# Four groups of two blocks, eight row buffers and half-megabyte weight units in a decoder step with PEER experts

## What is computed

```python
mod = silu(c) @ w_ada + b_ada                     # 6 vectors of 1024 for each condition
n = rmsnorm(x, g_mix) * (1 + sc1) + sh1
a_lin, a_gate, u, v, g_a, g_b = split(n @ w_in)   # 512, 512, 512, 512, 1024, 1024
a = silu(layernorm(causal_dwconv31(a_lin * sigmoid(a_gate)))) @ w_conv_out
b = (u * chunk_spatial_gate(layernorm(v))) @ w_gmlp_out
x = x + gt1 * ((sigmoid(g_a) * a + sigmoid(g_b) * b) @ w_out)
n2 = rmsnorm(x, g_ffn) * (1 + sc2) + sh2
# PEER: 8 heads, 2 x 128 keys, the 16 best of 16384 experts for each head and position
x = x + gt2 * sum_over_128_slots(softmax_gate * gelu(u_tab[eid] . n2) * v_tab[eid])
y = rmsnorm(x, g_final)
```

## Time and profile before

| | us |
|---|---|
| median of 3 runs | 3477.16 (3476.43 to 3483.25) |
| the profiled execution | 3482.56 |
| its span, from first to last instruction | 3480.8 |
| PE busy | 2028.8 (58%) |
| DVE busy | 2284.7 (66%) |
| ACT busy | 606.0 (17%) |
| POOL busy | 1220.7 (35%) |
| moved by DMA | 1231.43 MB, mean 354 GB/s |

### The profile page before, as it was taken

One profiled execution on the slowest core, in us unless ns is written; L12 is line 12 of the kernel. 1 busy time (PEld: TensorE's weight loads), 2 busy tenths in 40 slices (PEclk: granted clock), 3 DMA queues, 4 the chain that ended last, 5 costly groups with the idle time before them and its releaser, 6 DMA issues.

```text
span 3480.8 us, 27027 instructions
## 1 busy us (share of the span) xinstructions
PE 2028.8 (58%) x8700; PEld 885.6 (25%) x8700; DVE 2284.7 (66%) x5749; ACT 606.0 (17%) x1497; POOL 1220.7 (35%) x1046
## 2 busy tenths in 40 slices
PE   6998238576779533386666878733333433354333
PEld 4777204333455100033222444300000000010000
DVE  1524884875468978857865466897677676546555
ACT  1111311112121121212112121212121211111201
POOL 0000133332333344434432333345455444434442
PEclk7999659788889655598787989955555555555555
DMA  7543278988899988999998999999999999998998
GB/s 259 206 182 133 97 281 336 373 315 315 350 403 409 404 346 320 347 382 400 373 378 339 380 417 415 389 364 380 421 422 421 421 421 409 422 394 337 421 423 344
DMA packets 183773, 1231.43 MB, mean 354 GB/s; under 512 B 30496, under 2 KB 31136, under 8 KB 36176
## 3 DMA queue, kind: packets, MB, share of 16 engines
q0 software_dynamic: 148608, 1082.20, 77.2%
q1 hardware_dynamic: 35024, 147.52, 10.6%
HBM read 1220.62 MB, written 9.02 MB: 353 GB/s over the span
## 4 chain that ended last, share of the span: by engine, by line
PE 32%; DVE 29%; DMA 29%; ACT 4%; issue 3%; POOL 1%; SPq 1%; ACTq 0%; POOLq 0%; DVEq 0%
PE ps L605 18%; DMA big<-in_experts,eid 14%; DVE big L1587 9%; DMA w<-in_experts,eid 8%; PE ps L840 7%; DMA more_rows<-in_experts,eid 3%; PE ps L757 2%; ACT wd L1069 2%; DVE arena L1286 2%; DVE eid_s L1550 2%; PE ps L661 2%; DVE more_rows L1587 1%; DVE big L1228 1%; DVE wd L1602 1%; DVE arena L1548 1%
## 5 line engine op out<-in xcount | busy, mean ns | idle before, releaser
L1127 POOL DMA_INDIRECT big<-in_experts,eid x829 | 965.7, 1165 | 2121.4 <-PE ps L840 1569.2
L840 PE MATMUL ps<-big,wd 128*32 128x512 f32 x3316 | 825.7, 878 | 1051.7 <-DVE wd L1602 1043.8
L1587 DVE SCALAR_TENSOR_TENSOR big<-big,xr 128x1024 f32<-128x1024 f32 x829 | 1003.4, 1223 | 469.4 <-DMA big<-in_experts,eid 457.7
L1069 ACT ACTIVATE wd<-mask,act 128x32 f32<-128x32 f32 x1024 | 273.1, 313 | 2276.0 <-DVE big L1587 1763.0
L605 PE MATMUL ps<-big,wring 128*128 128x384 f32 (+2 forms) x1696 | 581.2, 494 | 89.1 <-issue 56.0
L840 PEld LDWEIGHTS ps<-big,wd 128*32 128x32 f32 x3316 | 94.8, 127 | 1594.2 <-DVE wd L1602 1526.2
L605 PEld LDWEIGHTS ps<-big,wring 128*128 128x128 f32 x1696 | 325.3, 198 | 360.8 <-issue 176.6
L1602 DVE TENSOR_TENSOR wd<-wd,gate 128x64 f32<-128x64 f32 x512 | 114.1, 223 | 271.1 <-ACT wd L1069 269.9
L840 PE MATMUL ps<-more_rows,wd 128*32 128x512 f32 x472 | 189.4, 891 | 141.9 <-DVE wd L1602 138.2
L1587 DVE SCALAR_TENSOR_TENSOR more_rows<-more_rows,xr 128x1024 f32<-128x1024 f32 x118 | 144.1, 1221 | 58.5 <-DMA more_rows<-in_experts,eid 57.9
L1286 DVE SCALAR_TENSOR_TENSOR arena<-arena,wdw 128x384 f32<-128x384 f32 (+1 forms) x360 | 182.2, 569 | 0.0
(11 more groups left out here) (241 smaller groups left out, 2091.1 us busy)
## 6 DMA issues: line engine op xcount, KB each, us to landing
wring<-in_w_in SPq DMA_DIRECT2D x40, 1024.0 KB
wring<-in_w_q SPq DMA_DIRECT2D x19, 1024.0 KB
big<-in_experts,eid POOLq DMA_INDIRECT x829
wring<-in_w_ada SPq DMA_DIRECT2D x12, 1024.0 KB
wring<-in_w_out SPq DMA_DIRECT2D x9, 1024.0 KB
big<-in_w_ada SPq DMA_DIRECT2D x6, 1024.0 KB, 7.0
xr<-in_w_ada SPq DMA_DIRECT2D x6, 1024.0 KB, 6.8
big<-in_w_in SPq DMA_DIRECT2D x4, 1024.0 KB, 14.0
```

The source lines that it names most:

```text
L840: mm = mmul(ps[QUAD * j:QUAD * (j + 1), half, :], wd[:, 2 * (at % 4) + jj, :], rows[jj][:, D + 512 * h:D + 512 * (h + 1)], start=(m == 0), ...
L1069: last = ac(wd[:, c + jj, :], mask[:], ACT.Gelu, scale=act[:, c + jj:c + jj + 1])
L1127: gp.indirect_dma_start(row(r), None, t["experts"], bass.IndirectOffsetOnAxis(ap=index, axis=0)).then_inc(s_row[r], 16)
L1587: last = v.scalar_tensor_tensor(out=row(r)[:, 0:D], in0=row(r)[:, 0:D], scalar=1.0, in1=x, op0=ALU.mult, op1=ALU.mult, accum_out=act[:, c: ...
```

## The change

STARTS becomes [0, 2, 4, 6]: groups of blocks 0 and 1, 2 and 3, 4 and 5, and 6 and 7 with the samples; their matmuls have 256, 256, 256 and 264 columns. There is one front more beside pairs, each now beside 128 pairs, and WIDE_AT moves from pair 320 to 384. nT, mT, the arena and the tables get smaller with the groups, and ROWS_1 goes from 7 to 8. The ring has six places of half a megabyte in place of three of one; for group 1 it has 14 in place of 7. Units of w_in and w_q are 128 columns, "out" units 256 columns; w_ada, w_out and the v columns of w_in are cut into an upper and a lower half of their rows, and both halves are awaited together. In a branch the order is in, out, in, and a gate unit's place is free when its gate matmuls are done rather than with the column block's last matmul. The planner is the same and gets other numbers.

```diff
@@ -39,10 +39,10 @@
 NSLOT = H * TOP
-RING = 3
-RING_1 = 7
-PIECE = 2048
-STARTS = [0, 2, 5]
+RING = 6
+RING_1 = RING + 8
+PIECE = 1024
+STARTS = [0, 2, 4, 6]
 NB1 = STARTS[-1]
...
@@ -51,7 +51,7 @@
 AW = max(NBG, NBL - 1) * P + W - 1
-ROWS_1, ROWS_2 = 7, 10
+ROWS_1, ROWS_2 = 8, 10
 LAST = len(STARTS)
...
@@ -301,40 +301,48 @@
 
+        def half_pieces(kind, src, i, done, count):
+            for rows in range(2):
+                pieces.append((kind, src, 2 * i + rows, done, count))
+
         def ada_pieces(lo, hi):
             for i in range(lo, hi):
                 ada_piece.append(len(pieces))
-                pieces.append(("ada", t["w_ada"], i, S["ada_mm"], i + 1))
+                half_pieces("ada", t["w_ada"], i, S["ada_mm"], i + 1)
 
 
         ada_pieces(0, 8)
         for g in GROUPS:
             ng = g.ng
             first_piece[g.n] = len(pieces)
+            for c in range(CC):
+                pieces.append(("in", w_in, 4 + c, *g.to("gate_mm", ng * (c + 1))))
+                pieces.append(("in", w_in, c, *g.to("lin_mm", ng * (c + 1))))
+            for c in range(CC):
+                pieces.append(("in", w_in, 8 + c, *g.to("u_mm", ng * (c + 1))))
             for half in range(2):
-                pieces.append(("in", w_in, 2 + half, *g.to("lin_mm", 2 * ng * (half + 1))))
-                pieces.append(("in", w_in, half, *g.to("lin_mm", 2 * ng * (half + 1))))
-            for half in range(2):
-                pieces.append(("in", w_in, 4 + half, *g.to("u_mm", 2 * ng * (half + 1))))
-            for half in range(2):
-                pieces.append(("in", w_in, 6 + half, *g.to("v_mm", g.nb)))
+                half_pieces("v", t["w_v"], half, *g.to("v_mm", g.nb))
             if g.n == 1:
                 ada_pieces(8, 16)
-            for base, wout, done in ((12, t["w_gmlp_out"], "ob_mm"), (8, t["w_conv_out"], "oa_mm")):
+            for base, wout, gated, done in ((24, t["w_gmlp_out"], "gb_mm", "ob_mm"), (16, t["w_conv_out"], "ga_mm", "oa_mm")):
                 for col in range(4):
-                    if col % 2 == 0:
-                        pieces.append(("out", wout, col // 2, *g.to(done, 2 * ng * (col + 2))))
-                    pieces.append(("in", w_in, base + col, *g.to(done, 2 * ng * (col + 1))))
-                if g.n == 1 and base == 12:
+                    pieces.append(("in", w_in, base + 2 * col, *g.to(gated, ng * (2 * col + 1))))
+                    pieces.append(("out", wout, col, *g.to(done, 2 * ng * (col + 1))))
+                    pieces.append(("in", w_in, base + 2 * col + 1, *g.to(gated, 2 * ng * (col + 1))))
+                if g.n == 1 and base == 24:
                     ada_pieces(16, 24)
             for i in range(4):
-                pieces.append(("wo", t["w_out"], i, *g.to("wo_mm", g.nb * (i + 1))))
-            for i in range(8):
-                pieces.append(("wq", t["w_q"], i, *g.to("q_mm", 2 * ng * (i + 1))))
+                half_pieces("wo", t["w_out"], i, *g.to("wo_mm", g.nb * (i + 1)))
+            for i in range(NCH):
+                pieces.append(("wq", t["w_q"], i, *g.to("q_mm", ng * (i + 1))))
 
         def piece(n):
-            k = CC if pieces[n][0] == "out" else KC
+            k = KC if pieces[n][0] in ("in", "wq") else KC // 2
             return home(n).rearrange("p (k n) -> p k n", k=k)
+
+        def rows_of(n, c):
+
+            return piece(n + c // (KC // 2))[:, c % (KC // 2), :]
 
...
@@ -350,9 +358,9 @@
                 return wring[:, slot * PIECE:(slot + 1) * PIECE]
-            if slot < RING + 2:
-                return big[:, (8 + 2 * (slot - RING)) * D:(10 + 2 * (slot - RING)) * D]
-            return xr[:, 2 * (slot - RING - 2):2 * (slot - RING - 1), :].rearrange("p a b -> p (a b)")
+            if slot < RING + 4:
+                return big[:, (8 + slot - RING) * D:(9 + slot - RING) * D]
+            return xr[:, slot - RING - 4, :]
 
...
@@ -501,20 +509,20 @@
                 load(n)
-                if pieces[n][0] == "wq" and pieces[n - 1][0] == "wo":
+                if pieces[n][0] == "wq" and pieces[n][2] == 3:
                     spill(g)
 
             def bring_x(g):
                 for b in g.blocks:
                     sp.dma_start(xn1[:, b, :], t["x"][b * P:(b + 1) * P, :]).then_inc(g.S["x_in"], 16)
 
-            for n in range(4, first_piece[2]):
+            for n in range(8, first_piece[2]):
                 with_spill(n, G1)
-                if n == 16:
+                if n == 32:
                     bring_x(GROUPS[1])
             for g in GROUPS[1:-1]:
-                for n in range(first_piece[g.n], first_piece[g.n + 1] + (3 if g.n == LAST - 1 else 0)):
-                    if n == first_piece[g.n] + 4 and g.n < LAST - 1:
+                for n in range(first_piece[g.n], first_piece[g.n + 1] + (RING if g.n == LAST - 1 else 0)):
+                    if n == first_piece[g.n] + 8 and g.n < LAST - 1:
                         bring_x(GROUPS[g.n])
...
@@ -526,9 +534,9 @@
                 sp.dma_start(x_first[0:w, b - NB1, :], t["x"][b * P:b * P + w, :]).then_inc(GL.S["x_in"], 16)
-            first_wo = max(n for n, p in enumerate(pieces) if p[0] == "wo") - 3
-            for n in range(first_piece[LAST] + 3, len(pieces)):
-                if n == first_piece[LAST] + 11:
+            first_wo = max(n for n, p in enumerate(pieces) if p[0] == "wo") - 7
+            for n in range(first_piece[LAST] + RING, len(pieces)):
+                if n == first_piece[LAST] + 16 + RING:
 
...
@@ -629,45 +638,45 @@
                     c, gi = i // ng, i % ng
-                    if i % (2 * ng) == 0:
+                    if gi == 0:
                         arrived(n)
                         arrived(n + 1)
                     if i >= 3:
                         pe.wait_ge(*g.to("a_done", i - 2))
-                    yield from tiles(n, (c % 2) * P, gi, ps[:, pair(i), 0:tg], s["gate_mm"])
-                    yield from tiles(n + 1, (c % 2) * P, gi, ps[:, pair(i) + 1, 0:tg], s["lin_mm"])
-                    if i % (2 * ng) == 2 * ng - 1:
+                    yield from tiles(n, 0, gi, ps[:, pair(i), 0:tg], s["gate_mm"])
+                    yield from tiles(n + 1, 0, gi, ps[:, pair(i) + 1, 0:tg], s["lin_mm"])
+                    if gi == ng - 1:
                         n += 2
                 yield from gap(5)
 
                 pe.wait_ge(*g.to("a_done", CC * ng))
                 for i in range(CC * ng):
                     c, gi = i // ng, i % ng
-                    if i % (2 * ng) == 0:
+                    if gi == 0:
                         arrived(n)
                     if i >= 6:
                         pe.wait_ge(*g.to("u_done", i - 5))
-                    yield from tiles(n, (c % 2) * P, gi, ps[:, 2 + i % 6, 0:tg], s["u_mm"])
-                    if i % (2 * ng) == 2 * ng - 1:
+                    yield from tiles(n, 0, gi, ps[:, 2 + i % 6, 0:tg], s["u_mm"])
+                    if gi == ng - 1:
                         n += 1
                 yield from gap(5)
 
                 pe.wait_ge(*g.to("u_done", CC * ng))
-                arrived(n)
-                arrived(n + 1)
+                for k in range(4):
+                    arrived(n + k)
                 for i, b in enumerate(g.blocks):
                     for half in range(2):
                         for c in range(KC):
                             mm = mmul(ps[0:width(b), 2 + i % 6, half * 256:(half + 1) * 256], nT[:, c, cols(b)],
-                                      piece(n + half)[:, c, :], start=(c == 0), stop=(c == KC - 1))
+                                      rows_of(n + 2 * half, c), start=(c == 0), stop=(c == KC - 1))
                             if (half, c) == (1, KC - 1):
                                 mm.then_inc(s["v_mm"], 1)
                             if c % 4 == 3:
                                 yield
-                n += 2
+                n += 4
                 if g.n == 1:
                     ada(8, 16)
-                    n += 8
+                    n += 16
                 yield from gap(12)
...
@@ -691,22 +700,21 @@
                         j, gi = i // ng, i % ng
-                        if i % (4 * ng) == 0:
-                            no = n
-                            arrived(no)
-                            n += 1
-                        if i % (2 * ng) == 0:
-                            arrived(n)
+                        if gi == 0:
+                            gate_piece = n + 2 * (j % 2)
+                            arrived(gate_piece)
+                            if j % 2 == 0:
+                                arrived(n + 1)
                         if i >= 3:
                             pe.wait_ge(*g.to(done, i - 2))
-                        yield from tiles(n, (j % 2) * P, gi, ps[:, pair(i), 0:tg], s[gate_sem])
-                        yield from tiles(no, (j % 4) * P, gi, ps[:, pair(i) + 1, 0:tg], s[out_sem], src, CC)
```

(47 more changed lines are left out.)

## The result

The changed kernel's median is 3432.9 us (3430.81 to 3434.69, 4 runs) against 3480.2 of the kernel before on the same chip: ratio 0.986, 95% interval 0.9839 to 0.9882, some 47 us less. The forecast was 3472 with 3450 to 3495 around it, and the range over all cases 3415 to 3535: the wide range held. The sum in the prediction had 5 us less than before (3475 for 3480), and 47 were measured. It also said that a measurement here can tell 7 us, so that it forecast no step that could have been told from none. 3432.9 lies outside the forecast's own range and inside that of rival 2 (3420 to 3449).

The account below looks back on a forecast made before the run. The DMA rate was taken as the limit, with the middle short of it. Group 1 432, fronts 776, 768 and 785, pairs alone 714 sum to 3475 against 3480; forecast median 3472, own range 3450 to 3495, 80% range 3415 to 3535.

Parts of the forecast that it names:

- rival 2: Front stages: buffer and units do more than forecast, so the kernel is faster, 3420 to 3449 us; chance 0.27.
- Bytes, +80: Weights: one more group reads 32 pieces of 1 MB once more, +80 us of DMA time.
- W: Loss in the fronts' matmul stretches: 22, 22 and 25 us forecast after the change.
- R: Loss in DVE-bound heads and tails of front stages: 109 us after, before 102; buffer takes 5 us per stage off.
- Stalls, 23 a front: Matmul stretches: PE's waits for weight pieces cost 23 us a front; half units with six slots remove all.
- Floors: DMA time of each front stage beside 128 pairs: 722 us, 2166 for three.
- Pairs alone: Last 132 pairs without a front: 714 us, with 3 us for two later routes otherwise hidden by ten buffers.
- Half units: Weight loads: 184 more DMA issues on SP, free except +2 us at the start; latency covered by the experts' queue.
- Rival 3: Weight loads: each unit costs DMA engine time, 184 more cost 17 us, 3489 us in all; chance 0.05.
- Group 1: First stage, without fetches: +2 us from four more SP issues ahead of the small loads, 432 us.
- The signs: Trace: fronts at 385 to 394 GB/s, no weight piece over 5 us in the chain, heads and tails all DVE.
- rival 1: Front stages: each pair still leaves DVE idle for rows as before, so slower, 3515 to 3552 us; chance 0.30.

Follow-up runs that it names:

- e6_eq_twice: The changed kernel with the routes' is_equal instruction issued twice each time; 3502.79 us, ratio 1.006 to the kernel before.
- e4_after_rows7: The changed kernel with seven row buffers instead of eight; 3474.77 us, ratio 0.9977 to the kernel before.
- e1_units: The changed kernel put back to groups [0, 2, 5] and seven row buffers, keeping the half-megabyte units; 3413.06 us, ratio 0.979 to the kernel before.
- e2_groups: The kernel before with only the groups changed to [0, 2, 4, 6]; 3545.49 us, ratio 1.0177 to the kernel before.
- e5_hist_late: The changed kernel with the four out_hist_s stores issued after all weights; 3426.73 us, ratio 0.9842 to the kernel before.

## Why the prediction was right, and which terms were off

Right was the wide range, which was drawn so that it takes in most of both rivals. The case that the forecast held likeliest (0.38, 3450 to 3495) did not come out.

- *Bytes, +80.* Right: 79 us. Groups alone cost 63, for W falls by 23 at the same time (158 to 135 in the table) and R rises by 8.
- *R, 109 less 15.* Right in cause (e6_eq_twice), 16 too low in size: 110. It was 121 before the buffer (e4_after_rows7), and the buffer took 11.
- *W, 69.* Too high: 37. The step that failed is the one that takes what was left in the last front (62 - 22 = 40 over 130 pairs) for the coupling of DVE and DMA and carries it over per pair as 28, 28 and 26, with a fifth off for the buffer. The 40 itself was right: with the stalls gone and seven buffers e1_units loses 38 in the same last front of three blocks and samples. But in fronts of two blocks e4_after_rows7 loses 20, 17 and 27, 64 where the forecast has 82. And the buffer took 27 of these where 13 were forecast. Why a narrower front loses less per pair, the runs do not separate.
- *Stalls, 23 a front.* Right on the new groups: 69 us in the three front stages from e2_groups to e4_after_rows7. On the old groups it was 40 and 25, so there the stalls of the front of blocks 2 to 4 cost more than the windows right behind one showed. By what way (the pairs held back, or the steps bunched behind) the runs do not separate. The other part of the loss was read too strongly from the earlier trace rows: of the six windows of 25 us in that front's matmul stretch in which PE is busy throughout, three have a DMA share of 0.75 to 0.80 and three of 0.89 to 1.01.
- *Floors.* The forecast charged 722 us of DMA to each front stage. The stages moved 905 MB, 2146 us at 421.5 GB/s, 20 less than three times 722. With W 32, the pairs alone 6, group 1 2, and R 16 the other way that closes the sum: 44 of the 45 us between 3475 and the span of 3430.
- *Pairs alone.* 714 forecast, 707.6 measured. That the two later routes beside them are hidden was wrong (e6), though it changed little in the sum, since the stage was 6 us shorter than forecast; how much of it was exposed before is not shown.
- *Half units.* Rival 3 asked what they cost in engine time. The hardware queue's share went from 10.6% of 3480.8 (369 us) to 13.7% of 3430.4 (470 us), and its bytes at 421.5 GB/s from 350 to 428: 19 us above the rate before, 42 after. So the packets do take some longer, but the time shows little of it: where nothing else is short, the matmul stretches after run at 419 GB/s where the full slices have 421.5. That is 0.6%, 9 us over the 1551 us of the three stretches: my estimate of the most that the units cost there. The Trainium skill (DMA: Bandwidth & Descriptors, Anatomy of one DMA) gives a DMA of the GpSimd path a fixed 2.0 us or so, and calls it mostly the latency of completion. Taken for these units too, and as time in which the engines stand still, it would be 368 us for 184 more, an estimate from that figure. This trace agrees with the page that it is latency: of the 368 us some 9 at most show, with a second queue beside.
- *Group 1.* Forecast +2, measured 430.3 against 428.2. That it agrees is luck: e4_after_rows7 and e5_hist_late, with the same front of group 1, have 427 and 426.
- *The signs.* The front stages run at 396, 400 and 388 GB/s where 385 to 394 were expected. One piece of a weight over 5 us is left in the chain, 18.15 us at 2208, behind the stores of the last front. In the first tail, from 1100 to 1167 us, the chain is DVE's with ACT between.

The rivals: coupling (rival 1) did not stay; DVE's idle for rows in the first front fell from 162 to 137 us for 127 pairs, in these two rows of the kernel after:

```profile
L1595 DVE SCALAR_TENSOR_TENSOR big<-big,xr 128x1024 f32<-128x1024 f32 x190 | 229.2, 1221 | 104.8 <-DMA big<-in_experts,eid 104.1
L1595 DVE SCALAR_TENSOR_TENSOR more_rows<-more_rows,xr 128x1024 f32<-128x1024 f32 x64 | 77.2, 1224 | 33.4 <-DMA more_rows<-in_experts,eid 33.1
```

Most of these 137 are only what a stage at the DMA's rate leaves: 298 MB take 707 us, and DVE has 544 of work and waits 52 for the gelu, so 111 would be left with no DMA time lost.

Rival 2 (0.27) is the case that came out: 3432.9 is in its range. In the first stage 752.6 is near its 748; in the second 759.6 is nearer to the forecast's 768; in the last 780.3 fits both (781 and 785).

## What to carry to other kernels

When one queue carries a fixed stream and a ring of weights runs beside it, look for the longest-held piece. Cutting the weights so that each place in the ring is freed by its own last reader was worth 70 us here in the same memory, at 9 us of DMA time at most; one more place for whole pieces was worth 52 to 55 for 1 MB more. Measure one buffer more and one less before paying for it with something else: here the regrouping that made room for the buffer cost 63 us for a gain of 41, while two ring places paid for it on the old groups, which came out 49 us ahead of the changed kernel. Where one engine sets a stretch, as DVE does around routes, every microsecond on it counts in full. Smaller units do not help there, and a buffer helps only at the turn to the next stretch, by 10 to 13 us over all fronts.

## What was not expected

Four small stores (120 KB each, in runs of 30 numbers) held SP's queue for some 55 us at issue, before and after, and moving them gained 6 us in one pair of kernels, where PE had waited behind them, and nothing in another, where it had not. And each part of the change was worth the same within 2 us in both settings in which it was measured, although all three act on the same stretch.
